# Two weight slots per product in the projections by token of a two-block transformer kernel

## The reference, cut to what matters

```
# first block, per layer (w_in: 1024 x 5704)
x = x + 0.5 * swiglu(rms_norm(x))
h = rms_norm(x)
u, va, q, k, v, qi, ki, wi, g_a, g_b = split(h @ w_in)
y_a  = gmlp_spatial(u, va) @ w_pa
y_b  = dsa_attention(rope(q), rope(k), v, rope(qi), rope(ki), wi) @ w_pb   # 64 keys per query by an index score
x = x + (sigmoid(g_a) * y_a + sigmoid(g_b) * y_b) @ w_out
x = x + 0.5 * swiglu(rms_norm(x))
# second block, per layer
h = rms_norm(x)
a_qkv, a_z, a_b, a_a, b_q, b_k, b_v = split(h @ w_in_2)
o_a = gated_delta_rule(...)          # uses a_qkv, a_b, a_a, a_z
o_b = dilated_attention(rope(b_q), rope(b_k), b_v)
x = x + rms_norm(concat(o_a, o_b) @ w_out_2)
x = x + rms_norm(conv_glu_ffn(rms_norm(x)))
```

## Time and profile before

| | profiled execution |
|---|---|
| span | 2197.8 us |
| TensorE matmul busy | 1992.1 us (91%) |
| TensorE weight load busy | 1943.5 us (88%) |
| VectorE / ScalarE / GpSimd busy | 1242.1 (57%) / 999.1 (45%) / 700.5 us (32%) |
| DMA engines, mean | 142 GB/s read over the span |
| matmuls by token, 128 x 256 moving | 1536 |
| mean granted TensorE clock | 0.949 |

### The profile page before, as it was taken

One profiled execution on the slowest core, in us unless ns is written; L12 is line 12 of the kernel. 1 busy time (PEld: TensorE's weight loads), 2 busy tenths in 40 slices (PEclk: granted clock), 3 DMA queues, 4 the chain that ended last, 5 costly groups with the idle time before them and its releaser, 6 DMA issues.

```text
span 2197.8 us, 42373 instructions
## 1 busy us (share of the span) xinstructions
PE 1992.1 (91%) x15702; PEld 1943.5 (88%) x15702; DVE 1242.1 (57%) x1541; ACT 999.1 (45%) x1323; POOL 700.5 (32%) x650
## 2 busy tenths in 40 slices
PE   6999989999999999889999799977999689879996
PEld 6999979999999999889999788967989689769996
DVE  5545565655456454756654565536664664356655
ACT  4434453544344344445443465445453363445543
POOL 5651301356327612112564214212230205122321
PEclk9999899999999998999999989989999799979998
DMA  6545433455455454333454522213445222124443
GB/s 224 191 138 193 154 116 133 141 187 192 152 186 198 151 193 159 116 134 135 174 196 149 169 97 96 78 41 114 161 146 192 95 102 91 39 77 153 169 153 136
DMA packets 49225, 314.37 MB, mean 143 GB/s; under 512 B 5712, under 2 KB 6864, under 8 KB 19920
## 3 DMA queue, kind: packets, MB, share of 16 engines
q1 hardware_dynamic: 48960, 311.09, 40.7%
q10 hardware_dynamic: 144, 1.69, 0.2%
HBM read 311.70 MB, written 1.05 MB: 142 GB/s over the span
## 4 chain that ended last, share of the span: by engine, by line
PE 59%; issue 25%; POOL 5%; DVE 4%; ACT 4%; DMA 1%; ACTq 1%; DVEq 1%; SPq 0%; POOLq 0%
PE ps L534 18%; PE ps L536 18%; PE ps L535 18%; PE ps L539 1%; PE ps L541 1%; PE ps L540 1%; DVE conv L1844 1%; ACT w_hi L1087 1%; ACT conv L1131 1%; POOL lev_c L2158 1%; DMA raw<-in_in_dram 1%; POOL m L2139 1%; POOL rope_tmp L2102 1%; DVE v L2014 0%; DVE rstd L1532 0%
## 5 line engine op out<-in xcount | busy, mean ns | idle before, releaser
L1526 DVE TENSOR_TENSOR w_lo<-raw,w_hi 128x2048 fp32r<-128x2048 f32 (+1 forms) x322 | 704.5, 2189 | 430.2 <-ACT w_hi L1087 428.3
L534 PE MATMUL ps<-xn,w_hi 128*128 128x256 f32 x2688 | 783.1, 291 | 65.6 <-DVE xn L1547 40.2
L535 PE MATMUL ps<-xn,w_hi 128*128 128x256 f32 x2688 | 771.4, 287 | 0.0
L536 PE MATMUL ps<-xn,w_lo 128*128 128x256 f32 x2688 | 771.0, 287 | 0.0
L1087 ACT ACTIVATE w_hi<-raw 128x2048 fp32r<-128x2048 f32 (+1 forms) x322 | 561.8, 1746 | 106.0 <-DMA raw<-in_down_dram 62.3
L534 PEld LDWEIGHTS ps<-xn,w_hi 128*128 128x128 f32 x2688 | 527.3, 196 | 78.8 <-DVE xn L1547 42.9
L535 PEld LDWEIGHTS ps<-xn,w_hi 128*128 128x128 f32 x2688 | 527.7, 196 | 0.6 <-issue 0.5
L536 PEld LDWEIGHTS ps<-xn,w_lo 128*128 128x128 f32 x2688 | 526.9, 196 | 0.0
L534 PE MATMUL ps<-h,w_hi 128*128 128x256 f32 x1056 | 301.2, 285 | 10.3 <-DVE conv L1844 5.7
L535 PE MATMUL ps<-h,w_hi 128*128 128x256 f32 x1056 | 300.1, 284 | 0.0
L536 PE MATMUL ps<-h,w_lo 128*128 128x256 f32 x1056 | 300.0, 284 | 0.0
(11 more groups left out here) (300 smaller groups left out, 2724.1 us busy)
## 6 DMA issues: line engine op xcount, KB each, us to landing
raw<-in_gu_dram SPq DMA_DIRECT2D x132, 1024.0 KB, 4.8
raw<-in_in_dram SPq DMA_DIRECT2D x70, 1024.0 KB, 4.8
raw<-in_down_dram SPq DMA_DIRECT2D x96, 704.0 KB, 4.1
raw<-in_out_dram SPq DMA_DIRECT2D x16, 1024.0 KB, 4.8
raw<-in_pb_dram SPq DMA_DIRECT2D x4, 1024.0 KB, 4.7
raw<-in_pa_dram SPq DMA_DIRECT2D x4, 1024.0 KB, 4.8
tables_all<-in_tables_dram ACTq DMA_DIRECT2D x1, 1648.0 KB, 6.9
rows<-in_rows_dram SPq DMA_DIRECT2D x2, 768.0 KB, 6.9
```

The lines of the kernel that those rows point to most:

```text
L534: pe.matmul(out, w, xh, start=first, stop=False)
L535: pe.matmul(out, w, xl, start=False, stop=False)
L536: return pe.matmul(out, wl, xh, start=False, stop=last)
L1526: dve.tensor_tensor(w_lo[:, r, 0:elems], raw[:, k % RAW_RING, 0:elems], w_hi[:, r, 0:elems], ALU.subtract).then_inc(lo.sem, 1)
```

## The change

`tokens` now takes two neighbouring slots j and j+1 together. The two places of the ring are viewed as 512 moving columns (2 x 256), so a chunk is three matmuls of 128 x 512 into a whole PSUM bank. A pair of slots is 48 matmuls in two halves t of 24. The pair waits for both slots' low parts at its start; `full` and `used` are raised by 2 at the end of the first and second half. Pairs alternate between banks 0, 1 and 2, 3 (`j % 4`).

A callback `then(q)` is run at four places of a pair: in the middle and at the end of each half. In the first block the side work of the even slot of a pair stands after the first half (q = 1), that of the odd slot after the second (q = 3), and `mean_square` after the first half of pair 0. In the second block `mid` of the even slot stands in the middle of the first half (q = 0), the later steps of the even slot after it (q = 1), `mid` of the odd slot in the middle of the second half (q = 2), the rest after it (q = 3).

On ScalarE the evictions are 128 x 512 and stand in the odd steps only. In the first block an odd step is: wait for the first half, evict it, split slot k+2, wait for the second half, evict it; an even step splits slot k+2 and evicts nothing. In the second block the split stays at the head of each step. The slots by feature that follow keep their form and use the other pair of banks (`shift`); the first of them waits for one eviction less.

```diff
-        def tokens(at, st, j, k_norm=None, between=None, prev=None):
+        def tokens(at, st, j, then, k_norm=None, prev=None):
 
-            whs, wls = slot(at, st, j)
+            pe.wait_ge(lo.sem, lo.upto(at, st.slot0 + j + 2))
+            r = (st.slot0 + j) % RING
+            wh = w_hi[:, r:r + 2].rearrange("p s (c n) -> p c s n", c=KC)
+            wl = w_lo[:, r:r + 2].rearrange("p s (c n) -> p c s n", c=KC)
             if prev is not None:
-                after(at, prev, j)
-            else:
-                pair(at, st, j)
...
+                after(at, prev, j // 2)
+            elif j >= 4:
+                pe.wait_ge(projected.sem, projected.upto(at, j - 2))
             for t in range(NT):
+                out = ps[:, j % 4 + t].rearrange("p (s n) -> p s n", s=2)
                 for c in range(KC):
                     if k_norm is not None and t == 0:
                         xn_ready(at, k_norm, c)
-                    last = mac_tok(ps[:, 2 * (j % 2) + t, 0:256], xn[:, c, 0, t * P:(t + 1) * P],
-                                   xn[:, c, 1, t * P:(t + 1) * P], wh[:, c], wl[:, c], c == 0, c == KC - 1)
-                last.then_inc(full.sem if t == 0 else used.sem, 1)
-                if between and t == 0:
-                    between()
+                    last = mac_tok(out, xn[:, c, 0, t * P:(t + 1) * P], xn[:, c, 1, t * P:(t + 1) * P],
+                                   wh[:, c], wl[:, c], c == 0, c == KC - 1)
+                    if c == KC // 2 - 1:
+                        then(2 * t)
+                last.then_inc((full if t == 0 else used).sem, 2)
+                then(2 * t + 1)
...
+            for k in range(0, 10, 2):
+                def then(q, k=k):
+                    if q == 1 and k == 0:
+                        mean_square(at, 1, True)
+                    if q % 2:
+                        projections_then(k + q // 2)
+                tokens(at, st1["in"], k, then, 0 if k == 0 else None, behind(st1["down1"]) if k < 4 else None)
+            for k in range(10, 20):
+                turn_of = {11: 0, 14: 2}
+                wide(at, st1["in"], k, 0, xn, KC, None,
+                     (lambda k=k: attend_turn(at, turn_of[k])) if k in turn_of else None, None, 3 if k == 10 else 1)
+                projections_then(k)
...
+            for k in range(0, 6, 2):
+                def then(q, k=k):
+                    (side_then if q % 2 else mid)(k + q // 2)
+                tokens(at, ss, k, then)
+            for k in range(6, 8):
+                wide(at, ss, k, 0, xn, KC, None, lambda: mid(k), None, 3 if k == 6 else 1)
+                side_then(k)
...
             for k in range(20):
-                split(at, si.slot0 + k + LEAD, 0, SLOT)
-                if k == 0:
+                if k == 1:
                     act.wait_ge(rstd_ok.sem, rstd_ok.upto(at, 2))
                 if k < 10:
                     for t in range(2):
...
+                        if k % 2:
+                            tile_done(act, at, si, k, t)
+                            part = (QI, Q, K, V, VA)[k // 2]
+                            f = ACT.Gelu_apprx_tanh if k >= 8 else ACT.Copy
+                            ins = act.activation(tok[:, part, t], ps[:, k // 2 % 2 * 2 + t], f,
+                                                 scale=rstd[:, T + t:T + t + 1])
+                        if t == 0:
+                            split(at, si.slot0 + k + LEAD, 0, SLOT)
+                    if k % 2:
+                        ins.then_inc(projected.sem, 2)
+                else:
+                    split(at, si.slot0 + k + LEAD, 0, SLOT)
```

More of the change, by code:

```diff
@@ L591, in behind, with wide @@
             return signals[st.free], st.free0 + st.pairs * st.free_by, st.free_by
-        def wide(at, st, j, g, x_of, chunks, k_norm=None, between=None, prev=None):
+        def wide(at, st, j, g, x_of, chunks, k_norm=None, between=None, prev=None, shift=0):
             whs, wls = slot(at, st, j, g)
@@ L603, in wide @@
                 elif f % 2 == 0:
-                    pair(at, st, q + 4 * g)
-                out = ps[:, 2 * (q % 2) + f % 2, 0:T]
+                    pair(at, st, q + 4 * g - shift // 2)
+                out = ps[:, 2 * ((q + shift) % 2) + f % 2, 0:T]
                 for c in range(chunks):
@@ L629, in down @@
             cycle(pe, st.pairs, 2, tile)
-        def tokens(at, st, j, k_norm=None, between=None, prev=None):
-            whs, wls = slot(at, st, j)
-            if prev is not None:
-                after(at, prev, j)
-            else:
-                pair(at, st, j)
-            wh = whs.rearrange("p (c n) -> p c n", c=KC)
-            wl = wls.rearrange("p (c n) -> p c n", c=KC)
+        def tokens(at, st, j, then, k_norm=None, prev=None):
[3 more added lines that the diff above has]
+            wl = w_lo[:, r:r + 2].rearrange("p s (c n) -> p c s n", c=KC)
+            if prev is not None:
+                after(at, prev, j // 2)
+            elif j >= 4:
+                pe.wait_ge(projected.sem, projected.upto(at, j - 2))
             for t in range(NT):
+                out = ps[:, j % 4 + t].rearrange("p (s n) -> p s n", s=2)
                 for c in range(KC):
@@ L758, in _, with projections_then @@
             pe.wait_ge(ready.sem, 16 * N_TABLES)
-            for k in range(20):
-                if k == 0:
[L761 to L771, removed]
+            def projections_then(k):
                 if k == 1:
@@ L970, in _, with side_then @@
             stage_open(at, sq)
[L971 to L975, removed]
+            def side_then(k):
                 if k == 0:
@@ L1438, in _ @@
                     level_copy(k - 1)
-                if k < 6:
+                if k < 6 and k % 2:
                     for t in range(2):
                         tile_done(act, at, ss, k, t)
[L1442 to L1446, removed]
+                        ins = act.activation(tok[:, (Q, K, V)[k // 2], t], ps[:, k // 2 % 2 * 2 + t], ACT.Copy,
+                                             scale=rstd[:, T + t:T + t + 1])
+                    ins.then_inc(projected.sem, 2)
+                if k >= 6:
                     act.wait_ge(projected.sem, projected.upto(at, k + 1))
@@ L1747, in _ @@
                         dst = u_t[:, f] if k < 12 else gates[:, f - WC]
-                        ins = dve.tensor_tensor(dst, ps[:, 2 * (k % 2) + t, 0:T], rstd[:, 0:T], ALU.mult)
+                        ins = dve.tensor_tensor(dst, ps[:, 2 * ((k + 1) % 2) + t, 0:T], rstd[:, 0:T], ALU.mult)
                     ins.then_inc(projected.sem, 1)
@@ L1968, in _ @@
                         tile_done(dve, at, ss, k, t)
-                        ins = dve.tensor_tensor(z_t[:, 2 * (k - 6) + t], ps[:, 2 * (k % 2) + t, 0:T], rstd[:, 0:T],
+                        ins = dve.tensor_tensor(z_t[:, 2 * (k - 6) + t], ps[:, 2 * ((k + 1) % 2) + t, 0:T], rstd[:, 0:T],
                                                 ALU.mult)
```

## The result

| | before | changed |
|---|---|---|
| median of 10 runs, us | 2201.61 (2195.88 to 2206.84) | 2210.80 (2208.36 to 2217.14) |
| the profiled execution and its span, us | 2199.98, 2197.8 | 2209.89, 2207.7 |
| mean granted clock in it | 0.949 | 0.945 |

The changed kernel takes 1.0048 times as long, 95% interval 1.0034 to 1.0061. The forecast was 2213, range 2203 to 2223. One more run of the kernel before, 2266.65 us at a granted clock of 0.815, is in none of the numbers here.

A forecast was written before the change was run, and what follows sets the result against it. TensorE, busy 91% of the span, was taken to bound the kernel. First block +14.4 and second block -2.0 made +12.4 us on an execution of 2199.98, stated as 2213 against the median, range 2203 to 2223.

The forecast's parts named there:

- turn: First block, TensorE's wait before 324.61 behind the attention mask chain: 7.2 us later per layer, part of the wait absorbed.
- The price of a product: TensorE's 512-column products start 0.227 us apart, by a fee of 0.013 per instruction; 9.9 us saved over 16 pairs.
- rival 1: 512-column products: two columns cost two columns, 0.240 us each, giving 2218; chance 0.2.
- The start: Stage "in", first block: pair 0 waits for slot 1's low part and starts 6.1 us later, the mean square 11.7 later.
- The small product: First block, behind the mean square: starts at 236.2, 6.9 us later, and runs at the low clock for 10.26 us.
- Rival 2: The small product stays at the high clock, up to 4.5 us less a layer, giving 2204; chance 0.15.
- My terms for the clock: First block: 2.2 us for low clock after the stops before pairs 0 and 8; up to 4.5 a layer at the small product.
- Pair 8: First block: waits for slot 9, starts 9.1 us later, ends 8.4 later; slot 11's split behind it delays the first mask 7.2.
- The second block: Six shorter halves where TensorE is alone save 1.0 us per layer, -2.0 in two layers.
- The evictions cost nothing: ScalarE: two evictions of 128 x 512 replace four of 128 x 256 at 45% load, at no cost.
- Rival 3: Not slower: the wait at 213.5 is hidden and the small product's start stays at 229.3; 2182 to 2190; chance 0.08.
- Rival 4: The clock: each of three first-block stops could cost 2.2 us more than set, 13 in all, giving 2225; chance 0.07.

The follow-up runs named there:

- e14: The kernel before with pairs in the second block alone, its first block exactly as before: 2201.04 us, ratio 1.0006.
- e12: The kernel before with slots 8 and 9 split right behind the index sums and the second `top_k` moved behind the first two attention masks: 2185.90 us, ratio 0.9942.
- e9: The changed kernel with 45 products of 256 columns that nobody reads issued ahead of pair 0's wait: 2213.91 us, ratio 1.0059.
- e2: The changed kernel with slots 8 and 9 taken singly again: 2210.28 us, ratio 1.0046.
- e5: The changed kernel with slot 1 split before the last square and residual of the previous stage instead of behind them: 2198.44 us, ratio 0.9992.
- e4: The changed kernel with the first block's ten slots by token taken singly, wide evictions kept, second block still paired: 2205.95 us, ratio 1.0026.

## Why the prediction was right, and where not

The sign, the size and the first mechanism were right; that the sum came so close is in part luck, as shown below. Step by step:

| step | predicted | profile after |
|---|---|---|
| distance of 512-column products | 0.227 | 0.22 to 0.23 |
| stop before pair 0, its start | 6.0, 219.6 | 6.07, 219.66 |
| first half of pair 0 (5.45 + 2.2) | 7.65 | 8.31 |
| small product, start | 236.2 | 236.47 |
| small product, length | 10.26, low clock | 7.86, clock 0.67 |
| pair 2 (10.9 + 1.4) | 12.3 | 13.42, clock 0.81 |
| relu of the second scores | +5.6 | +4.9 |
| waits at pairs 2, 4, 6 | none | none |
| pair 8: wait, start | 12, 297.9 | 11.00, 297.54 |
| first half of pair 8 (5.45 + 2.2) | 7.65 | 7.01 |
| first mask | +7.2 | +5.9 |
| turn | +7.2, wait 3.2 | +5.9, wait 2.85 |
| first block | +14.4 | +14.3 |
| second block | -2.0 | -4.4 |

**The price of a product** was right, and with it the reading of 0.12 us at 256 columns as a fee of 0.013 per instruction. It had been a choice: the fp32 row, 0.22, lay nearer to 0.216. 256 columns more do not bring more of the fee, so rival 1 (0.240) falls. The rule of the Trainium skill ("TensorE: Matmul & The Clock Gate", section "Back-to-back issue gap"), 0.216 at this width, is 0.011 below the 0.227 that the timeline shows; the trace does not agree with its 2.5 ns. The section gives that formula for an isolated matmul; for a stream of weight loads and matmuls, which this is (14934 of each), it gives 131 ns at 512 columns, and the trace, with 227, agrees with that still less.

**The start.** The text says that the mean square comes 11.7 later; its own times of the root, 217.82 and 228.5, make 10.7, and the sum went on from 228.5. The root came at 229.05, 11.2 later.

**The small product** ran half at the high clock: the step that failed is "I let it run at the low clock again". Rival 2, with half its weight, was true there, 2.4 us, but pair 2 behind it met a lower clock and took 1.1 back (13.42 for 12.3). So the string of VectorE was 4.9 late where 5.6 was forecast, and the turn 5.9 for 7.2. That the block still ends at +14.3 for +14.4 is luck. Behind the turn another 1.4 us is lost, in the products of the merge (`yb`), which ran wholly at the high clock in the profile of before and did not in this one. e14, whose first block is that of before, loses as much there in layer 0, and e12, without pairs, in both layers; so it does not take the change to lose it. The windows of these 96 products, before and e14:

```profile
389.82:401.43 11.61, 11.61 (x96) 11.61 (x97) 6.87 (x9) 9.54 (x15) 0.00 (x0) 1.00 0.50 179
392.30:405.30 13.00, 13.00 (x96) 13.00 (x96) 6.71 (x9) 10.27 (x16) 0.00 (x0) 0.87 0.44 161
```

My terms for the clock, 2.2 at each of two stops and 4.5 between rivals, priced single stops; in e9, what one stop did not cost, later ones did.

**Pair 8** was right in its numbers and mostly wrong in its weight on the path. I wrote that the first mask is late because pair 8 ends late and ScalarE splits slot 11 behind it. That path is there, but it sets only the last 0.64 us, the time that VectorE waits for ScalarE before slot 11. The rest of the mask's +5.9 is VectorE's own string, +5.2 already at slot 8. The string is late because the relu is, and that because pair 0 and the small product are. e2 (wait 3.6 shorter, 0.5 us gained) and e5 (wait the same, all gained) show it. With the string back in place, in e5, the path through pair 8 is worth more, 2.1 us in layer 0 and 0.7 in layer 1. What makes the change slower than before is then that slot 1 is split too late for pair 0; whether pair 8 eats some of what e5 could have gained on top is not measured.

**The second block** was priced at -2.0 by the products. The profile shows -1.0 in stage "side" of the first layer, as worked out, and e14 shows that nothing of it is left at the end. The rest of the 4.4 in the profile lies behind that stage, most of it (+13.3 to +11.2 in the first layer) between products that the change does not touch. So this term's mechanism was right in the stage, and what it adds at the end lies, by e14's interval (0.9992 to 1.0019), between -1.8 and +4.2 us.

**"The evictions cost nothing"** failed in e4, which stays 0.26% above before with the pairs of block 1 undone. In the changed kernel it does not show by itself, since the same chain is late by more at its head. e4's profile gives it about 1 us at slot 8, and no run takes the evictions alone.

**Rival 3**, not slower if pair 0's wait is hidden, was put at 2182 to 2190. e5 is nearly this case (no stop over 1.3 us before pair 0, the small product 1.2 late), and it gave 2198.4: the condition decides the sign, but the price was not right, since 10 to 18 us of shorter products were to come out of a stream that waits for VectorE anyway. **Rival 4** did not come about as a larger sum.

## What to carry to other kernels

Before a step is made to need two inputs at once, look where the second is produced, and move that first: here six microseconds of lateness per layer outweighed all that 768 saved instructions could bring, and one line earlier would have hidden most of them. A wait of 11 us on the busiest engine can be worth almost nothing (here 3.6 us less of it brought 0.5): what it hangs on and what the next wait hangs on may be one string, and only shortening that string (here, moving eight rounds that the next consumer did not need) moves the end. Test this by taking one wait away and watching whether the next one grows by as much.

## What the runs showed of the hardware

**The granted clock is most of the scatter.** Over 67 runs of the kernel before, beside the experiments, the time goes with the mean granted clock (correlation -0.87): six runs at 0.942 have a mean of 2207.5 us, eleven at 0.950 have 2196.8, between them 1.3 us for each 0.001. The changed kernel's ten runs have a mean of 0.944, those 67 of 0.946. So one profile can be 6 us off another of the same instructions (e14's block 1), and differences of a few microseconds between two profiles are read with both clocks beside them, or from many runs.

**Keeping the engine busy ahead of a stop moved the low clock, and did not remove it.** In e9 the filler took 5.4 of 6.1 idle us; the clock stayed at 1.00 there, and fell to 0.66 for 0.74 at the next long stop, and the ratio did not come down (1.0059 for 1.0048). The wide product at the low clock starts every 0.427 us, which is 512 columns at 1.2 GHz, without the extra 0.013 that it has at the high clock (0.227 for 0.213).
